# Routing stage of a two-block transformer with experts: order of evictions, exponentials and the gates' table, and wide sums in the last norm

## The chip, the cores and the metric

One core of one Trainium2 chip. The metric is the device time of one execution of the whole program in microseconds, lower is better; several executions are made and their median is taken.

## The reference

512 tokens of width 1024, all in float32. A first block (latent attention with a Fourier branch, then a squared-ReLU MLP) is followed by a second one: a mixer of a convolution and an mLSTM, and a hierarchical mixture of 32 experts, of which each token takes two. The change touches only the seam between the mixer and the experts:

```
h   = x * rsqrt(mean(x*x) + eps) * norm_ffn_g            # the last norm but one
grp = argmax(h @ rg_w + rg_b); p_grp = its softmax value  # 4 groups
top2 of the 8 expert logits of that group
gate = p_grp * softmax(top2)                              # two weights per token
for each expert e, over its tokens xs:
    ys = (silu(xs @ w_gate[e]) * (xs @ w_up[e])) @ w_down[e]
out[token] += gate * ys
y = rmsnorm(x + out)
```

## The kernel before, in words

Every engine has its own program, a hand-written order of instructions, and they wait for each other on counted semaphores. A float32 product is made of three products in a faster form: ScalarE rounds an operand (its high half), VectorE takes the remainder (its low half), and TensorE multiplies high by high, low by high and high by low. Weights are streamed in units of 1 MB: SyncE loads a unit into a raw buffer once VectorE has finished with the unit that was there, `convert(n)` on ScalarE (line 1538) writes its high half, `convert(n)` on VectorE (line 2201) its low half. `use(n)` converts all units up to `n + ahead`. The half buffers are a ring too: a conversion waits until TensorE has used the unit that was in the buffer. From expert 0 on the units come in the order gate 0, up 0, gate 1, down 0, up 1, gate 2, down 1, up 2 and so on, two units each; the expert part is one product stream of 24 (gate), 24 (up) and 24 (down) matmuls of 512 columns per expert.

The seam runs in this order.

- Stage "out2". The mixer's last projection makes xT, the token stream with features on partitions, one block of 128 features (m = 0 to 7) at a time (line 1344). After each block come 4 products for the router's logits (`logits`, line 1363, 36 columns) and 4 for the tokens times the norm's gain, turned to token-major (`gained`, line 1375, 128 columns); ScalarE evicts the latter into hN (line 1590). In the profile each of these float32 products shows as two instructions. `total(12)` (lines 686 and 691) sums the squares over partitions: 8 products of one column, with `oneD` (1/1024) as the moving operand, and ScalarE's `root(12)` (line 1560) takes the root. `token_major(m)` turns xT itself (line 1383): ScalarE copies the eight results into xN (line 1590).
- Stage "route", TensorE: `fill(b, n)` (line 621) is n products of 128 columns with ones whose result nobody reads; then the positions of each token in its expert's list (lines 1412 to 1416), `token_major(3)`, `table(0)` (3 fills, then the table of indices, line 1426), `token_major(4..7)`, and `table(1)`, the table of gates. The PSUM banks are eight in rotation, so the transposes 6 and 7 wait for ScalarE's copies of 0 and 1.
- Stage "route", ScalarE: scales hN by the root's reciprocal in four row blocks and stores each (lines 2091 and 2093, the scratch from which tokens are gathered); loads the exponential's table and takes two exponentials (lines 2095, 2096); converts the second unit of gate 0 and the first of up 0; copies xN; stores xN as the running sum (2 MB, line 2117).
- Stage "route", VectorE: logits, top 2 and one-hot rows (lines 2979 to 3000, many through the helper line 2310), the table's operands R1, the indices `idt`; then the gates' values from the exponentials, converts the second unit of gate 0, counts overflow blocks, and evicts the gates' table.
- Stage "moe": `turn_x(x)` turns the gathered tokens of expert x on TensorE (line 1444), ScalarE copies the high half (line 1590), VectorE takes the low half (line 2310); `half_mm` (line 1460) makes the gate and up products, ScalarE's sigmoid (line 2127) and VectorE make the activations, `turn_a` (line 1469) turns them, `down` (line 1487) multiplies, ScalarE scales by the gate (line 2141), and GpSimd adds the rows to the sum in memory (line 3242). GpSimd also gathers the tokens (line 3231), four experts ahead; the first gather waits for the indices, the stored hN and the norm's reciprocal, the next ones also for transposes 3, 5 and 7.
- SyncE (line 3277) loads in unit order, with extra waits: the second unit of gate 1 waits for gather 0, the first unit of down 0 waits until the stored sum has landed (its buffer lies over xN), and the first load into the fifth raw buffer waits for the gates' table.

```
if n == U_E["g", 1][1]:
    p.wait_ge(*done("dma", "xg", 0))
if n == FIFTH:
    p.wait_ge(*done("dve", "tab", 1))
if n == U_E["d", 0][0]:
    p.wait_ge(*done("dma", "od"))
```

Of the kernel before, what the change touches and what calls it, by code (L numbers as in the profile page):

```python
# [6 lines left out]
F32 = mybir.dt.float32  # L7
# [4 lines left out]
ALU = mybir.AluOpType  # L12
ACT = mybir.ActivationFunctionType
AX = mybir.AxisListType
# [137 lines left out]
class Book:  # L152
# [25 lines left out]
    def done(self, *key):  # L178
        if key == (None,):
            return None, 0  # L180
        if not self.real:
            return None, 0
        name, n = self.value[key]
        return self.sem(name), n
# [74 lines left out]
def build(nc, A, out, ctx):  # L259
# [4 lines left out]
    done = book.done  # L264
# [347 lines left out]
    def pe_program(p):  # L612
        e = p.e
        ps.restart()

        def fill(b, n):

            p.wait_ge(*done("pool", "one"))
            p.wait_ge(*done(*b.before))
            for _ in range(n):  # L620
                e.matmul(b.t[:, 0:128], one1[:, :], one1[:, :], start=True, stop=True)
# [52 lines left out]
        def total(n):  # L674

            width = NORMS[n][1]
            apart = n > 1
            b = ps.take(("norm", n), ("act", "rs", n))
            if n == 0:
                fill(b, 22)  # L680
            p.wait_ge(*done("dve", "sqa", n, 6 if apart else 7))
            p.wait_ge(*done("pool", "one"))
            p.wait_ge(*done(*b.before))
            last = width // 128 - 1
            for i in range(width // 128):
                ins = e.matmul(b.t[:, i:i + 1], sqs[:, i * 128:(i + 1) * 128], oneD[:, 0:1], start=(i == 0),
                               stop=(i == last and not apart))
            if apart:
                p.wait_ge(*done("act", "sq", n, 7))
                for i in range(width // 128):  # L690
                    ins = e.matmul(b.t[:, i:i + 1], scr[:, 1, i * 128:(i + 1) * 128], oneD[:, 0:1], start=False,
                                   stop=(i == last))
            ins.then_inc(*p.inc("sum", n, 7))

# [724 lines left out]
        def table(k, n, vals):  # L1419
            b = ps.take(("tab", k), ("dve", "tab", k))  # L1420
            if k == 0:
                fill(b, 3)
            p.wait_ge(*done("dve", "R", k))
            p.wait_ge(*done(*b.before))
            for c in range(8):
                ins = e.matmul(b.t[:, 0:n], R1[:, c, :], vals[:, c, :], start=(c == 0), stop=(c == 7))
            ins.then_inc(*p.inc("tab", k))
# [2 lines left out]
        table(0, 32, Ot)  # L1430
        for m in range(4, 8):
            token_major(m)
        table(1, 64, Og)


        p.stage("moe")
# [1 line left out]
        def turn_x(x):  # L1438
            for q in range(2):
                b = ps.take(("x4", x, q), ("dve", "xL", x, q))  # L1440
                p.wait_ge(*done("dma", "xg", x))
                p.wait_ge(*done(*b.before))
                for d in range(4):
                    ins = e.transpose(b.t[:, d * 128:(d + 1) * 128], xg[x % NXG][:, (4 * q + d) * 128:(4 * q + d + 1) * 128], ident)  # L1444
                ins.then_inc(*p.inc("x4", x, q))

        def half_mm(x, what, h):
            r = x % 2
            n = U_E[what, x][h]
            u = units[n]  # L1450
            b = ps.take(("e" + what, x), ("dve", what, x)) if h == 0 else ps["e" + what, x]
            if x == 0 and what == "g" and h == 0:
                fill(b, 7)
            p.wait_ge(*done("dve", "xL", x, 1))
            p.wait_ge(*done("dve", "lo", n))
            p.wait_ge(*done(*b.before))
            for k in range(4):
                kk = 4 * h + k
                for i, (l, w) in enumerate(tri((xH[r][:, kk, :], xL[r][:, kk, :]), (u.hi[:, k, :], u.lo[:, k, :]))):
                    ins = e.matmul(b.t[:, :], l, w, start=(kk == 0 and i == 0), stop=(kk == 7 and i == 2))  # L1460
            ins.then_inc(*p.inc("use", n))
# [30 lines left out]
        turn_x(0)  # L1492
        half_mm(0, "g", 0)
        half_mm(0, "g", 1)
        turn_x(1)
        for x in range(NEXP):
            half_mm(x, "u", 0)
# [23 lines left out]
    def act_program(p):  # L1521
# [3 lines left out]
        def convert(n):  # L1525
            u = units[n]
            at_[0] = n + 1
            if not u.split:
                return
            p.wait_ge(*done("dma", "u", n))  # L1530
            for key in u.half_keys:
                p.wait_ge(*done(*key))
            if HOLD.get(n):
                p.wait_ge(*done("pe", HOLD[n]))
            if n in AFTER:
                for key in AFTER[n]:
                    p.wait_ge(*done(*key))
            e.activation(u.hi, u.raw, ACT.Copy).then_inc(*p.inc("hi", n, on="hi"))  # L1538
# [17 lines left out]
        def root(n):  # L1556
            nd, width, _, place = NORMS[n]
            nt = width // 128
            p.wait_ge(*done("pe", "sum", n, nd - 1))
            e.activation(rcol[:, 4 * place:4 * place + nt], ps["norm", n].t[:, 0:nt], ACT.Sqrt, bias=eps[:, :]).then_inc(  # L1560
                *p.inc("rs", n))
# [508 lines left out]
        for m in range(8):  # L2070
# [9 lines left out]
                root_next(12)  # L2080
            if m:
                gained(m - 1)
        root(12)
        gained(7)


# [3 lines left out]
        for i in range(4):  # L2090
            e.activation(hN[:, i, :], hN[:, i, :], ACT.Copy, scale=rcol[:, i:i + 1]).then_inc(*p.inc("hN", i))
            p.wait_ge(*done("act", "hN", i))
            e.dma_start(hd_[i * 128:(i + 1) * 128, :], hN[:, i, :]).then_inc(*p.land("hd", "hd", i))
        p.wait_ge(*done("dve", "ee"))
        e.activation(ee, ee, ACT.Exp).then_inc(*p.inc("ee"))
        e.activation(dd, dd, ACT.Exp).then_inc(*p.inc("dd"))
        convert(U_E["g", 0][1])
        convert(U_E["u", 0][0])
        for m in range(8):
            token_major(m)  # L2100
        p.also("mid")
# [4 lines left out]
        def turn_x(x):  # L2106
            r = x % 2
            for q in range(2):
                p.wait_ge(*done("pe", "x4", x, q))
                if x > 1:  # L2110
                    p.wait_ge(*done("pe", "use", U_E["u", x - 2][1]))
                else:
                    p.wait_ge(*done("pe", "out2", 7))
                copy(xH[r][:, 4 * q:4 * q + 4, :], ps["x4", x, q].t[:, :].rearrange("p (d c) -> p d c", d=4), p.inc("xH", x, q))

        p.wait_ge(*done("act", "xN", 7))
        e.dma_start(od.rearrange("(i p) d -> p i d", p=P), xN[:, :, :]).then_inc(*p.land("od"))
        turn_x(0)
        for n in U_E["g", 0]:
            use(n)  # L2120
        turn_x(1)
# [69 lines left out]
    def dve_program(p):  # L2191
# [3 lines left out]
        def convert(n):  # L2195
            u = units[n]
            at_[0] = n + 1
            if not u.split:
                return
            p.wait_ge(*done("act", "hi", n))  # L2200
            e.tensor_tensor(u.lo, u.raw, u.hi.bitcast(F32), ALU.subtract).then_inc(*p.inc("lo", n, on="lo"))  # L2201
# [104 lines left out]
        def copy(out_, in_, by):  # L2306
            e.tensor_copy(out_, in_).then_inc(*by)

        def TT(out_, a, b, op, *key):
            e.tensor_tensor(out_, a, b, op).then_inc(*p.inc(*key))  # L2310

        def TS(out_, a, s1, s2, op0, op1=None, key=()):
            if op1 is None:
                e.tensor_scalar(out_, a, s1, None, op0).then_inc(*p.inc(*key))
            else:
                e.tensor_scalar(out_, a, s1, s2, op0, op1).then_inc(*p.inc(*key))
# [705 lines left out]
            *p.inc("tab", 0))  # L3022
        p.wait_ge(*p.own())
        copy(idt[:, 0:32], tv[:, 1, :], p.inc("idt"))
        p.wait_ge(*done("act", "dd"))
        e.tensor_reduce(pg, ee, AX.X, ALU.add).then_inc(*p.inc())
        TS(gk[:, 0, :], dd, 1.0, None, ALU.add)
# [9 lines left out]
        copy(Og[:, :, 0:32], Og8, p.inc())  # L3037
        p.wait_ge(*p.own())
        TT(Og[:, :, 32:64], Og8, Og[:, :, 0:32].bitcast(F32), ALU.subtract, "R", 1)
        convert(U_E["g", 0][1])  # L3040
        TS(nov, cnt, 128.5, None, ALU.is_gt)
        for lim in (256.5, 384.5):
            TS(oi, cnt, lim, None, ALU.is_gt)
            p.wait_ge(*p.own())
            TT(nov, nov, oi, ALU.add)
            p.wait_ge(*p.own())
        e.tensor_reduce(ovf[:, 0:1], nov, AX.X, ALU.add).then_inc(*p.inc())
        p.wait_ge(*p.own())
        copy(ovi[:, 8:9], ovf[0:1, 0:1], p.inc("ovi"))
        gates_ = ps["tab", 1].t  # L3050
        p.wait_ge(*done("pe", "tab", 1))
        copy(gsl[:, 0:32], gates_[:, 0:32], p.inc())
        p.wait_ge(*p.own())
        TT(gsl[:, 0:32], gsl[:, 0:32], gates_[:, 32:64], ALU.add, "tab", 1)


        p.stage("moe")
        ahead = 3
        p.stage("moe")
        ahead = 3  # L3060

        def turn_x(x):
            r = x % 2
            for q in range(2):
                p.wait_ge(*done("act", "xH", x, q))
                TT(xL[r][:, 4 * q:4 * q + 4, :], ps["x4", x, q].t[:, :].rearrange("p (d c) -> p d c", d=4),
                   xH[r][:, 4 * q:4 * q + 4, :].bitcast(F32), ALU.subtract, "xL", x, q)

        turn_x(0)
        for n in U_E["g", 0]:  # L3070
            use(n)
        turn_x(1)
        def silu(x):
            r = x % 2
            p.wait_ge(*done("act", "sig", x))
# [527 lines left out]
```

## Time and profile before

| what | value |
|---|---|
| median of 3 executions | 1684.21 us (1683.75 to 1687.3) |
| the profiled execution | 1685.23 us |
| its span, first to last instruction | 1683.4 us |
| mean granted TensorE clock | 0.987 |
| TensorE busy | 1624.3 us (96%) |
| VectorE busy | 1269.6 us (75%) |
| ScalarE busy | 921.3 us (55%) |
| GpSimd busy | 255.3 us (15%) |
| moved by DMA | 322.92 MB, mean 192 GB/s |

All rows come from one profiled execution. Times are microseconds from the start of its span. PE is TensorE's matmuls, PEld its weight loads, DVE is VectorE, ACT ScalarE, POOL GpSimd and SP SyncE. "Granted clock" is the share of TensorE's full 2.4 GHz that the chip granted. Matmuls are pipelined: two that follow each other overlap in the timeline, so a row's duration there is a little longer than its place on the chain of waits. A "releaser" is what the profile infers to have ended a wait. The page divides the span in 40 slices; DMA share is the mean busy share of the core's 16 DMA engines.

### The profile page before, as it was taken

What the parts mean: (1) busy time and instruction counts of PE and PEld (TensorE: products, weight loads), DVE (VectorE), ACT (ScalarE), POOL (GpSimd) and SP (SyncE); (2) the same over time, 40 slices, a digit from 0 to 9 for tenths busy, and PEclk for the clock granted to TensorE, in tenths of its full rate; (3) what the DMA queues carried; (4) which work ended last, traced back from release to release, by engine and by line L of the source; (5) the groups of instructions that cost most, each with busy time, mean ns of one, the idle gap of its engine ahead of it and who ended that gap; (6) DMA issues with size and microseconds to landing.
All of it is one profiled execution on the core that took longest, in us unless ns stands there. A gap on an engine that the chain in (4) does not pass through costs nothing.

```text
span 1683.4 us, 20485 instructions
## 1 busy us (share of the span) xinstructions
PE 1624.3 (96%) x8376; PEld 1332.3 (79%) x8376; DVE 1269.6 (75%) x1457; ACT 921.3 (55%) x1070; POOL 255.3 (15%) x176
## 2 busy tenths in 40 slices
PE   6999999999999999999999999999999999999994
PEld 3768876657988989898888677888888888888883
DVE  6554876777667847474799974589999999999994
ACT  6433235443443625252633234588888887888884
POOL 0000021000028333310000100102112122121200
PEclk9999999999999999999999999899999999999997
DMA  9206821003222313131222111399999999999993
GB/s 381 81 4 242 301 90 76 0 0 126 76 100 76 127 74 129 72 134 67 79 98 76 38 39 56 131 380 414 374 386 369 378 369 369 364 378 363 383 361 115
DMA packets 54484, 322.92 MB, mean 192 GB/s; under 512 B 12529, under 2 KB 13041, under 8 KB 17778
## 3 DMA queue, kind: packets, MB, share of 16 engines
q1 hardware_dynamic: 42192, 304.76, 47.3%
q0 software_dynamic: 9216, 8.43, 2.2%
q10 hardware_dynamic: 2978, 8.37, 1.3%
q8 instruction: 68, 1.11, 0.3%
q14 instruction: 30, 0.25, 0.0%
HBM read 323.60 MB, written 23.07 MB: 206 GB/s over the span
## 4 chain that ended last, share of the span: by engine, by line
PE 87%; DVE 6%; ACT 3%; DMA 3%; issue 1%; POOL 0%; SPq 0%; ACTq 0%; POOLq 0%; DVEq 0%
PE ps L584 25%; PE ps L1460 20%; PE ps L1487 10%; PE ps L1088 7%; PE ps L774 3%; PE ps L750 2%; PE ps L1020 2%; PE ps L1344 2%; DVE scr L2511 2%; PE ps L1444 2%; PE ps L808 1%; ACT whi L1538 1%; DVE wlo L2201 1%; DMA xT<-in_x 1%; PE ps L880 1%
## 5 line engine op out<-in xcount | busy, mean ns | idle before, releaser
L2201 DVE TENSOR_TENSOR wlo<-raw,whi 128x2048 fp32r<-128x2048 f32 x256 | 583.8, 2302 | 129.1 <-ACT whi L1538 129.0
L1538 ACT ACTIVATE whi<-raw 128x2048 fp32r<-128x2048 f32 x256 | 485.7, 1911 | 155.1 <-PE ps L584 40.9
L1460 PE MATMUL ps<-whi,xH 128*128 128x512 f32 x512 | 203.0, 396 | 0.0
L1460 PE MATMUL ps<-whi,xL 128*128 128x512 f32 x512 | 200.3, 391 | 0.0
L1460 PE MATMUL ps<-wlo,xH 128*128 128x512 f32 x512 | 199.6, 390 | 0.0
L584 PE MATMUL ps<-hH,whi 128*128 128x512 f32 x352 | 138.8, 394 | 0.3 <-ACT dmax L2014 0.3
L584 PE MATMUL ps<-hH,wlo 128*128 128x512 f32 x352 | 137.2, 390 | 0.0
L584 PE MATMUL ps<-hL,whi 128*128 128x512 f32 x352 | 137.1, 389 | 0.0
L3242 POOL DMA_INDIRECT sum_scratch<-yb,idt x32 | 51.1, 1596 | 451.2 <-ACT yb L2141 416.9
L1460 PEld LDWEIGHTS ps<-whi,xL 128*128 128x128 f32 x512 | 96.2, 188 | 20.8
L1460 PEld LDWEIGHTS ps<-wlo,xH 128*128 128x128 f32 x512 | 96.4, 188 | 19.2
L1460 PEld LDWEIGHTS ps<-whi,xH 128*128 128x128 f32 x512 | 96.4, 188 | 19.1
L1487 PE MATMUL ps<-whi,aH 128*128 128x512 f32 x256 | 102.3, 400 | 0.6 <-DVE aL L2310 0.6
L1487 PE MATMUL ps<-wlo,aH 128*128 128x512 f32 x256 | 99.8, 390 | 0.0
L1487 PE MATMUL ps<-whi,aL 128*128 128x512 f32 x256 | 99.7, 390 | 0.0
L2773 DVE SCALAR_TENSOR_TENSOR acc<-up,vec,acc 128x512 f32<-128x512 f32 x110 | 82.4, 750 | 2.9
L3231 POOL DMA_INDIRECT xg<-h_scratch,idt x32 | 70.0, 2188 | 94.9 <-DVE gk L2310 84.8
L584 PEld LDWEIGHTS ps<-hH,wlo 128*128 128x128 f32 x352 | 66.1, 188 | 14.1
L584 PEld LDWEIGHTS ps<-hH,whi 128*128 128x128 f32 x352 | 66.1, 188 | 13.9 <-ACT dmax L2014 0.4
L584 PEld LDWEIGHTS ps<-hL,whi 128*128 128x128 f32 x352 | 66.1, 188 | 13.6 <-issue 0.2
L584 PE MATMUL ps<-UH,whi 128*128 128x512 f32 x176 | 68.5, 389 | 0.0
L584 PE MATMUL ps<-UL,whi 128*128 128x512 f32 x176 | 68.5, 389 | 0.0
(517 smaller groups left out, 3542.0 us busy)
## 6 DMA issues: line engine op xcount, KB each, us to landing
raw<-in_experts SPq DMA_DIRECT2D x192, 1024.0 KB, 7.7
raw<-in_streamed SPq DMA_DIRECT2D x92, 1024.0 KB, 4.8
xT<-in_x SPq DMA_DIRECT2D x1, 2048.0 KB, 17.3
h_scratch<-hN ACTq DMA_DIRECT2D x4, 512.0 KB, 2.6
sum_scratch<-xN ACTq DMA_DIRECT2D x1, 2048.0 KB, 13.3
out<-Y SPq DMA_DIRECT2D x4, 512.0 KB, 2.7
ctxT<-in_ctx SPq DMA_DIRECT2D x1, 1024.0 KB, 20.1
Y<-sum_scratch SPq DMA_DIRECT2D x2, 512.0 KB, 5.9
```

Of the source, the lines that this page charges most:

```text
L584: ins = e.matmul(o, l, r, start=(i == 0), stop=(i == len(prs) - 1))
L750: ins = e.matmul(b.t[0:mw, hs(h)], l, r, start=(k == 0 and i == 0), stop=(k == 7 and i == 2))
L774: ins = e.matmul(b.t[:, :], l, r, start=(k == 0 and i == 0), stop=(k == nk - 1 and i == 2))
L1020: ins = e.matmul(b.t[:, :], V[:, j, h // 2, s_:s_ + 2, :].rearrange("p s c -> p (s c)"), PT[h % 2][:, j, :], start=(j == 0), stop=(j == 5))
L1088: ins = e.matmul(bank.t[:, hs(half)], l, r, start=(k == 0 and i == 0), stop=(k == 3 and i == 2))
L1460: ins = e.matmul(b.t[:, :], l, w, start=(kk == 0 and i == 0), stop=(kk == 7 and i == 2))
L1487: ins = e.matmul(bs[q].t[:, :], l, w, start=(kk == 0 and i == 0), stop=(kk == 3 and i == 2))
L1538: e.activation(u.hi, u.raw, ACT.Copy).then_inc(*p.inc("hi", n, on="hi"))
L2201: e.tensor_tensor(u.lo, u.raw, u.hi.bitcast(F32), ALU.subtract).then_inc(*p.inc("lo", n, on="lo"))
L2773: e.scalar_tensor_tensor(out=acc[:, m, :], in0=up[:, m, j:j + 512], scalar=wc, in1=acc[:, m, :], op0=ALU.mult, op1=ALU.add).then_inc(*p.in ...
L3231: e.indirect_dma_start(out=xg[r], out_offset=None, in_=hd_[:, :], in_offset=bass.IndirectOffsetOnAxis(ap=idt[:, x:x + 1], axis=0), bounds_ ...
L3242: e.indirect_dma_start(out=od[:, :], out_offset=bass.IndirectOffsetOnAxis(ap=idt[:, x:x + 1], axis=0), in_=yb[x % 3], in_offset=None, boun ...
```

## The change

Four edits, in the seam only.

1. `total(12)`: the sums of the last norm ahead of the experts are 128 columns wide (every column the same), with `oneK` (1/128) as the moving operand. ScalarE's root reads one column of each 128 and multiplies by 0.125.
2. ScalarE converts only the second unit of gate 0 ahead of the eight copies of xN; the exponentials and the first unit of up 0 come behind the copies of expert 0's turned tokens.
3. VectorE makes the gates' values and evicts their table later: expert 0's low halves go ahead of them; the conversion of the second unit of gate 0 and the count of overflow blocks follow the indices directly.
4. TensorE makes the gates' table behind the gate products of expert 0. Fills: 7 instead of 3 ahead of the indices' table, 9 new ones ahead of expert 0's transposes, 5 instead of 7 ahead of its gate products.

```diff
@@ total(n), TensorE
+            cw, one = (128, oneK[:, :]) if n == 12 else (1, oneD[:, 0:1])
             for i in range(width // 128):
-                ins = e.matmul(b.t[:, i:i + 1], sqs[:, i * 128:(i + 1) * 128], oneD[:, 0:1], start=(i == 0),
+                ins = e.matmul(b.t[:, cw * i:cw * i + cw], sqs[:, i * 128:(i + 1) * 128], one, start=(i == 0),
                                stop=(i == last and not apart))
...
@@ table(k, n, vals), TensorE
             if k == 0:
-                fill(b, 3)
+                fill(b, 7)
...
         for m in range(4, 8):
             token_major(m)
-        table(1, 64, Og)
...
@@ turn_x(x), TensorE
+                if x == 0 and q == 0:
+                    fill(b, 9)
                 p.wait_ge(*done("dma", "xg", x))
...
@@ half_mm, TensorE
             if x == 0 and what == "g" and h == 0:
-                fill(b, 7)
+                fill(b, 5)
...
         turn_x(0)
         half_mm(0, "g", 0)
         half_mm(0, "g", 1)
+        table(1, 64, Og)
         turn_x(1)
@@ ScalarE
-        root(12)
+        p.wait_ge(*done("pe", "sum", 12, 7))
+        e.activation(rcol[:, 0:4], ps["norm", 12].t[:, :].rearrange("p (i c) -> p i c", i=4)[:, :, 0], ACT.Sqrt,
+                     bias=eps[:, :], scale=0.125).then_inc(*p.inc("rs", 12))
...
-        p.wait_ge(*done("dve", "ee"))
-        e.activation(ee, ee, ACT.Exp).then_inc(*p.inc("ee"))
-        e.activation(dd, dd, ACT.Exp).then_inc(*p.inc("dd"))
         convert(U_E["g", 0][1])
-        convert(U_E["u", 0][0])
         for m in range(8):
             token_major(m)
...
         turn_x(0)
+        p.wait_ge(*done("dve", "ee"))
+        e.activation(ee, ee, ACT.Exp).then_inc(*p.inc("ee"))
+        e.activation(dd, dd, ACT.Exp).then_inc(*p.inc("dd"))
         for n in U_E["g", 0]:
             use(n)
         turn_x(1)
@@ VectorE (only the order of the pieces changes)
         copy(idt[:, 0:32], tv[:, 1, :], p.inc("idt"))
+        convert(U_E["g", 0][1])
+        (count of overflow blocks: 8 instructions)
+        turn_x(0)
         p.wait_ge(*done("act", "dd"))
         (the gates' values: 8 instructions, the last makes Og)
-        convert(U_E["g", 0][1])
-        (count of overflow blocks: 8 instructions)
+        for n in U_E["g", 0]:
+            use(n)
+        turn_x(1)
         (eviction of the gates' table: 2 instructions)
-        turn_x(0)
-        for n in U_E["g", 0]:
-            use(n)
-        turn_x(1)
```

## Rows read from the trace of the kernel before

**Rows 1.** Chain of waits from 1055 to 1170 us: start, us, what.

```profile
1066.26 0.97 PE ps L1375 x8
...
1068.02 0.89 PE ps L691 x8
...
1092.69 5.93 PE ps L1460 x24
...
1102.46 10.92 DMA raw<-in_experts
...
1148.24 5.46 PE ps L1487 x24
```

**Rows 2.** Timeline of TensorE: start, us, instruction, count, idle before and its releaser.

```profile
1069.67 2.06 PE L1375 MATMUL ps<-gdiag,xT 128*128 128x128 f32 x8
...
1073.60 3.74 PE L621 MATMUL ps<-one 128*128 128x128 f32 x32
...
1077.17 0.20 PE L1412 MATMUL ps<-AS,triB 128*128 128x32 bf16 x2
...
1080.07 1.07 PE L1426 MATMUL ps<-Ot,R 128*128 128x32 f32 x8 [1.24 <-DVE R L2310]
...
1084.41 1.97 PE L1383 MATMUL ps<-cst,xT 128*128 128x128 f32 x8 [2.33 <-ACT xN L1590]
...
1098.45 1.04 PE L1444 MATMUL ps<-cst,xg 128*128 128x128 f32 x8
...
1130.24 0.50 PE L1487 MATMUL ps<-whi,aH 128*128 128x512 f32 x1 [0.61 <-DVE aL L2310]
```

**Rows 3.** Waits of SyncE's queue, and the store of the sum (KB, us to landing).

```profile
SPq L3277 <- DMA sum_scratch<-xN: 14.3, 1, 14.3
...
sum_scratch<-xN ACTq DMA_DIRECT2D x1, 2048.0 KB, 13.3
```

**Rows 4.** Stretches: us, PE, PEld, DVE, ACT, POOL busy (count), PEclk, DMA share, GB/s.

```profile
1070.00:1072.00 2.00, 2.00 (x11) 2.00 (x11) 1.76 (x11) 0.24 (x1) 0.00 (x0) 0.50 0.00 0
...
1088.00:1090.00 2.00, 2.00 (x11) 2.00 (x11) 0.82 (x3) 0.86 (x2) 1.18 (x2) 0.50 1.01 410
...
1101.00:1102.00 1.00, 1.00 (x6) 0.83 (x5) 1.00 (x1) 0.98 (x3) 0.00 (x0) 1.00 0.00 0
...
1104.00:1110.00 6.00, 6.00 (x30) 4.85 (x29) 5.67 (x5) 5.07 (x4) 0.00 (x0) 1.00 1.01 429
```

**Rows 5.** Timeline of VectorE.

```profile
1076.08 0.29 DVE L2310 TENSOR_TENSOR AS<-O 128x128 bf16<-128x128 f32 x1
...
1081.63 0.18 DVE L2307 CAST idt<-tv 128x32 uint32<-128x32 f32 x1
...
1083.73 2.28 DVE L2201 TENSOR_TENSOR wlo<-raw,whi 128x2048 fp32r<-128x2048 f32 x1
```

**Rows 6.** Timeline of ScalarE.

```profile
1078.67 1.28 ACT L2095 ACT_TABLE_LOAD   x1 [0.39 <-ACT hN L2091]
...
1080.18 3.69 ACT L1538 ACTIVATE whi<-raw 128x2048 fp32r<-128x2048 f32 x2
1083.78 3.98 ACT L1590 ACTIVATE xN<-ps 128x512 f32<-128x512 f32 x8
```

**Rows 7.** The first gather, and landings of the issues at 1082.72 and at 1084.45.

```profile
1082.72 1.43 POOL L3231 DMA_INDIRECT xg<-h_scratch,idt  x1 [84.81 <-DVE gk L2310]
...
DMA to landing us min/median/max: 3.1/3.1/3.1
...
DMA to landing us min/median/max: 12.3/12.3/12.3
```

**Rows 8.** DMA packets of 1084.5 to 1085 (first row), and by queue of 1093 to 1094.

```profile
DMA packets 136, 0.00 MB, mean 9 GB/s; under 512 B 135, under 2 KB 135, under 8 KB 136
...
q1 hardware_dynamic: 29, 0.24, 69.8%
q10 hardware_dynamic: 27, 0.11, 26.8%
```

More of the change, by code:

```diff
@@ L690, in total @@
                 for i in range(width // 128):
-                    ins = e.matmul(b.t[:, i:i + 1], scr[:, 1, i * 128:(i + 1) * 128], oneD[:, 0:1], start=False,
+                    ins = e.matmul(b.t[:, cw * i:cw * i + cw], scr[:, 1, i * 128:(i + 1) * 128], one, start=False,
                                    stop=(i == last))
@@ L3024, in dve_program, with turn_x @@
         copy(idt[:, 0:32], tv[:, 1, :], p.inc("idt"))
+        convert(U_E["g", 0][1])
+        TS(nov, cnt, 128.5, None, ALU.is_gt)
+        for lim in (256.5, 384.5):
+            TS(oi, cnt, lim, None, ALU.is_gt)
+            p.wait_ge(*p.own())
+            TT(nov, nov, oi, ALU.add)
+            p.wait_ge(*p.own())
+        e.tensor_reduce(ovf[:, 0:1], nov, AX.X, ALU.add).then_inc(*p.inc())
+        p.wait_ge(*p.own())
+        copy(ovi[:, 8:9], ovf[0:1, 0:1], p.inc("ovi"))
+        p.stage("moe")
+        ahead = 3
+        p.stage("moe")
+        ahead = 3
+        def turn_x(x):
+            r = x % 2
+            for q in range(2):
+                p.wait_ge(*done("act", "xH", x, q))
+                TT(xL[r][:, 4 * q:4 * q + 4, :], ps["x4", x, q].t[:, :].rearrange("p (d c) -> p d c", d=4),
+                   xH[r][:, 4 * q:4 * q + 4, :].bitcast(F32), ALU.subtract, "xL", x, q)
+        turn_x(0)
         p.wait_ge(*done("act", "dd"))
@@ L3039, in dve_program @@
         TT(Og[:, :, 32:64], Og8, Og[:, :, 0:32].bitcast(F32), ALU.subtract, "R", 1)
-        convert(U_E["g", 0][1])
[L3041 to L3049, printed above, removed]
+        for n in U_E["g", 0]:
+            use(n)
+        turn_x(1)
         gates_ = ps["tab", 1].t
@@ L3054, in dve_program @@
         TT(gsl[:, 0:32], gsl[:, 0:32], gates_[:, 32:64], ALU.add, "tab", 1)
[L3057 to L3067, printed above, removed]
-        turn_x(0)
-        for n in U_E["g", 0]:
-            use(n)
-        turn_x(1)
         def silu(x):
```

## The prediction

> **What bounds it now.** I read the page first: TensorE is busy nearly all of the span, so a gain must take idle or slow time off TensorE, or the transfers that feed it. The change touches only the routing stretch, 1066 to about 1130 us, so I read the chain of waits there. It runs through the first gate products (from 1092.69), then a weight landing of 10.92 us, ScalarE's roundings of weights, and VectorE's lower half of the turned activations, for which the down products of expert 1 wait until 1130.24 [rows 1]. TensorE idles only 0.61 us there [rows 2], and behind it I find no stall: that product's start is where I settle the sum.
>
> Why is a landing on the chain? SyncE stands 14.3 us in front of the first down-weight load, because that load overwrites the token-major sum, whose 2 MB store is issued at 1087.8 and lands 13.3 us later [rows 3]. The four loads behind it go out together from 1101.13. The DMA engines are full at 1088, idle in the microsecond from 1101 (0.00) and then full, at 429 GB/s [rows 4]. So from 1102 on landings come at DMA rate, one load (1.05 MB) in about 2.5 us; an expert's six need 15, its 72 products 16.4 (24 in 5.46 [rows 1]) and the transposes more, so the stream catches up, but not at once. The stream of loads that feeds expert 1 starts when the store has landed, and that sets 1130.24.
>
> TensorE's own loss is ahead of it. Its clock is granted at 0.50 (1.2 GHz) at 1070 to 1072 and again around 1088, at 1.00 (2.4 GHz) later [rows 4]. Eight token transposes take 1.97 us busy at the half level and 1.04 at the full one [rows 2].
>
> **The change, part by part.**
>
> *Wide sums.* 16 one-column products become 128 columns wide. A 128-column run of 8 takes 0.97 us on the chain; the sums take 0.79 (from its end to 1068.02) and 0.89 [rows 1]. So 1.94 replaces 1.68: +0.26 before the root, and as the last logits then run at 0.81 rather than 0.95, +0.12 on VectorE's routing chain. What they may buy is the clock, which falls directly behind them. I take it as held: it fell behind 16 products of one column and recovered under 128-column work, with the fills from 1073.60 at 3.74/32 = 0.12 each [rows 2, 4]. Then the last gain products (2.06 busy) save 0.9 us, the 12 transposes about 0.7, and the 16 filling products end near 1075.9 instead of 1077.17. The position products waited for these fills: their input was ready at 1076.37 [rows 5]. Now they wait for it at 1076.5. Gain on the routing chain 0.6 us, bounds 0.6 gained and 0.3 lost (clock not held). The index table ends at 1081.2 instead of 1081.81. The fills ahead of it grow from 3 to 7, 8 more passes at 0.12, under 1.0 us; TensorE idled 1.24 there [rows 2], so they cost nothing; at the half level they would cost 1.
>
> *VectorE.* The gates' chain, from the index's end at 1081.81 to 1083.73 (the two overlap by 0.1), goes behind the turned tokens, so the low half of the second gate unit starts 2.0 + 0.6 = 2.6 us sooner and ends at 1083.4 [rows 5]. That frees a raw buffer, and SyncE's first load of the pair (now 1086.04) goes out at 1083.5. The second waits for the first gather, due at 1085.2.
>
> *ScalarE.* The row scaling follows the last gain eviction and moves 0.8 us ahead. The table load (1.28) and both exponentials leave, and of two roundings (3.69 together) only one stays: the eight token evictions, 3.98 us from 1083.78, run from 1079.8 to 1083.8 [rows 6]. TensorE can supply them: the last four transposes follow the index table at 1080.5 and no longer wait 2.33 us for a bank [rows 2]. The store of the sum goes out at 1083.8, 3.9 sooner.
>
> *TensorE.* It waits for gather 0. That was issued at 1082.72 and took 3.1 us [rows 7]; 0.6 sooner it lands at 1085.25. 9 fills (2.1 us) cover the wait. Transposes at full clock to 1086.1, ScalarE's two copies (0.60 each) and VectorE's 0.69 behind them give a start of the gate products at 1087.8, against 1092.3. 5 fills (1.2 us) cover that. At 5.46 us for 24 products they end at 1093.25, against 1098.45: 5.2 gained. Now the gates' table comes, about 0.9 at the full level (1.07 busy for the narrower one). Its input needs the exponentials: ScalarE ends its second copy at 1086.9, loads the table and finishes at 1088.5; VectorE's 2.1 us then end at 1090.6, 2.6 before TensorE asks. On TensorE the second expert's transposes and all up products stand behind that wait; on VectorE the up weights' low halves. Who wants the gate values (ScalarE's scaling of the first outputs, SyncE's first load into the fifth raw buffer) asks after 1110, and they are there by 1100. Behind the exponentials stand the roundings of expert 0's up weights; the first unit's low half is ready at 1092.9, needed at 1095. Gather 1, which took 12.3 us behind the same loads [rows 7], should land near 1094, as TensorE reaches it. So the up products start at 1095.0 against 1099.2 (the second expert's transposes begin at 1098.45 [rows 2]): 4.2 gained on TensorE, and without the old stall it would reach the down products of expert 1 at 1125.4.
>
> *The transfers.* They decide between 1125.4 and later. The same four megabytes of weights and sum, and the gathers, must pass before the sum has landed. Their start moves with the first load, by 2.6 us; if the engines stay full the end moves as much. The other bound is the store's own 13.3 us from its issue: 3.9. The load that was second of the pair now follows the store, but with 8 packets per engine against the store's 32 it should be through first if the queues share. I take 2.8, near the first, because rows show the engines full. So the sum lands at 1098.3, the four loads follow, the last lands at 1110.6 instead of 1113.37, and ScalarE and VectorE, whose chain from there is unbroken, deliver at 1127.4.
>
> The rows on sharing: the store's packets begin 4 to 5 us after its issue, behind the weights' queue; at 1093 both run evenly, 29 and 27 packets in one microsecond [rows 8]. The Trainium skill (DMA: Bandwidth & Descriptors, Queues, rings and completion order) says an engine goes round between the queues that have work. The later mix agrees, the late first packet does not, so a transfer that is new to a busy engine seems to wait. By the rule alone a late gather 0 (below) would be served in turn.
>
> **Sum.** TensorE alone 4.8 gained (4.2 and the old 0.6), transfers 2.8: the smaller counts. The profiled execution took 1685.23 us (span 1683.4 and 1.8 around it): 1682.4. The median of the runs, 1684.21, is 1.0 below that execution, so I give 1681.4. TensorE's idle ahead of the down products of expert 1 grows from 0.61 to about 2 (with perhaps 0.5 of it at expert 0's). A measurement here tells a change of about 0.2%, 3.4 us, from none.
>
> **Rivals.**
>
> *A. TensorE is the bound.* If the store passes ahead of the second weight load, it lands 4.8 or more sooner and TensorE arrives last: 4.8 gained, 1679.4. For: the store's issue moves 3.9 and overtakes that load. Against: it has 512 packets of its own behind a busy engine. 20%.
>
> *B. The clock does not hold.* The stretch from 1080 to 1087 still holds narrow table products, transposes and a wait. At the half level the transposes cost 0.9 more, 5 fills 1.1, and the first gate products 1.4: TensorE arrives at 1128.8, gain 1.4: 1682.8. For: it fell in this stretch before, with 2.33 and 1.24 us of idle. Against: the fills. 17%.
>
> *C. Gather 0 is caught by the loads: slower.* It landed in 3.1 us; the next one, behind loads, took 12.3 [rows 7]. Its packets run just before the first load's, which now begin near 1084.9. Caught, it lands at 1094.5; TensorE sits idle, its clock falls, the gate products end at 1104.7 against 1098.45, and with the table's 0.9 behind them and the old 0.61 absorbed the down products start 6.6 later: 1690.8. It decides from a landing about 4.8 us late, or 2 to 3 if the clock falls too; up to 2 late costs nothing. Against: its 144 packets are mostly 4 bytes and were gone in half a microsecond, some 0.5 us ahead of the loads' new start [rows 8]. 8%.
>
> *D. The wide sums do nothing:* the index comes 0.3 later, the stream starts 1.7 sooner instead of 2.6, gain about 1.8, 1682.4. 5%.
>
> **Chances.** Forecast (gain 2.0 to 3.6) 50%. Over 3.4 us lie three tenths of it (15%), most of A (17%) and a little else (2%): faster 0.34. C: slower 0.08. The rest within 0.2%: 0.58. The range runs from A with a little noise, 1679.0, to a loss of 0.8, 1685.0; C and a larger gain are outside.
>
> **What would show it.** Clock 1.00 from 1066 to 1130; position products near 1076.6; the transposes' wait of 2.33 gone; gate products from 1087.8; the store issued near 1083.8 and landed near 1098; DMA share again near zero just ahead of the four loads, at about 1098 instead of 1101; a wait on VectorE's activations of 1 to 2 us at about 1126; behind it 17.7 us per expert as now. Wrong, if the stall stays under 0.7 (A), if a 0.50 stands at 1083 to 1090 (B), or if the first gather takes over 5 us (C).

## The result, and the profile after

The changed kernel is slower: 1688.39 us median of 20 executions (1685.71 to 1690.75) against 1684.46 of 20 of the kernel before, ratio 1.0019 (95% interval 1.0013 to 1.0026), 3 to 4 us. I had forecast 1681.4 and given this side 8%.

The profiled execution's span is 1686.2 us against 1683.4. Its routing stretch begins 0.9 us earlier for reasons ahead of the change, so I compare stretches: from the first of block 6's router logits (1065.28 before, 1064.39 changed) to expert 1's first down product (1130.24 before [rows 2], 1132.88 changed). That is 64.96 us before and 68.49 now, 3.5 more, which is the result. Behind it both kernels run the same 17.7 us per expert.

The timeline of TensorE in the changed kernel (columns as in [rows 2]; line numbers are one to five higher than before):

```profile
1068.78 1.14 PE L1376 MATMUL ps<-gdiag,xT 128*128 128x128 f32 x8
1069.75 1.47 PE L1384 MATMUL ps<-cst,xT 128*128 128x128 f32 x12
1071.06 3.74 PE L621 MATMUL ps<-one 128*128 128x128 f32 x32
1075.50 0.21 PE L1413 MATMUL ps<-AS,triB 128*128 128x32 bf16 x2 [0.70 <-DVE AS L2314]
...
1078.41 1.07 PE L1427 MATMUL ps<-Ot,R 128*128 128x32 f32 x8 [0.34 <-DVE R L2314]
1079.32 1.96 PE L1384 MATMUL ps<-cst,xT 128*128 128x128 f32 x16
1081.12 2.17 PE L621 MATMUL ps<-one 128*128 128x128 f32 x18
1090.65 1.97 PE L1446 MATMUL ps<-cst,xg 128*128 128x128 f32 x8 [7.36 <-DMA xg<-h_scratch,idt]
```

The first half is as forecast: the last gain products take 1.14 us instead of 2.06, the position products now wait 0.70 for their input instead of for the fills, and the wait of 2.33 for a bank is gone. Then TensorE stands 7.36 us in front of gather 0. The chain of waits and, below it, GpSimd's and VectorE's timelines and ScalarE's issue of the store at that place:

```profile
1081.06 9.55 DMA xg<-h_scratch,idt
```

```profile
1081.06 2.41 POOL L3235 DMA_INDIRECT xg<-h_scratch,idt  x1 [84.03 <-PE ps L1384]
1080.06 2.28 DVE L2205 TENSOR_TENSOR wlo<-raw,whi 128x2048 fp32r<-128x2048 f32 x1
1082.71 0.38 ACTq L2118 DMA_DIRECT2D sum_scratch<-xN  x1
```

Gather 0 takes 9.55 us to land instead of 3.1, and GpSimd's instruction for it 2.41 instead of 1.43 [rows 7]. VectorE's low half now stands directly behind the indices and runs beside it. The packets by queue (packets, MB, share of the DMA engines) in the microseconds from 1085, 1087 and 1089 (q1 is SyncE's loads, q10 ScalarE's store, q0 the gathers):

```profile
q1 hardware_dynamic: 42, 0.34, 104.0%
...
q1 hardware_dynamic: 25, 0.13, 49.9%
q10 hardware_dynamic: 32, 0.13, 31.8%
q0 software_dynamic: 11, 0.00, 0.6%
...
q10 hardware_dynamic: 96, 0.39, 95.4%
q0 software_dynamic: 97, 0.00, 6.4%
```

GpSimd is done at 1083.47, yet nothing of gather 0 moves before 1087: first the load's packets, then the gather's in equal number with the store's. Meanwhile the clock falls (the microseconds from 1085 and 1087; columns as in [rows 4], here without the engines):

```profile
1085.00:1086.00 1.00, 1.00 1.04 344
...
1087.00:1088.00 1.00, 0.50 0.82 262
```

So the transposes take 1.97 us again instead of 1.04, and the first gate products run at the half level. They start 30.0 us after the logits' start (1094.40), against 27.1 before: 3.0 of the 3.5 us are lost by then. Behind them TensorE waits for nothing until the down products.

### The profile page after: what moved, and what is told of

Read it like the earlier page. It is cut to its first block, busy times and chain, and to the rows that moved or that the text cites. A ratio compares the mean times of both kernels' runs of the same rounds, so it can differ in the third digit from the quotient of the medians.

```text
span 1686.2 us, 20528 instructions
## 1 busy us (share of the span) xinstructions
PE 1621.0 (96%) x8398; PEld 1331.5 (79%) x8398; DVE 1268.9 (75%) x1457; ACT 920.9 (55%) x1070; POOL 255.0 (15%) x176
## 4 chain that ended last, share of the span: by engine, by line
PE 88%; DVE 6%; DMA 3%; ACT 2%; issue 1%; POOL 0%; SPq 0%; POOLq 0%; DVEq 0%; ACTq 0%
PE ps L584 26%; PE ps L1462 21%; PE ps L1489 10%; PE ps L1089 7%; PE ps L775 3%; PE ps L751 2%; PE ps L1021 2%; PE ps L1345 2%; PE ps L1446 2%; DVE scr L2515 2%; PE ps L809 1%; DMA xT<-in_x 1%; PE ps L1471 1%; PE ps L881 1%; DVE wlo L2205 1%
```

## The experiments

Each kernel was executed 10 or 11 times in turn with the kernel before, except the two that are marked as one execution. "Stretch" is as defined above; the ratios are to the kernel before, with 95% intervals. The first three take away one thing at a time of what stands in front of gather 0.

**Only the load waits.**

```diff
-            if n == U_E["g", 1][1]:
+            if n in U_E["g", 1]:
                 p.wait_ge(*done("dma", "xg", 0))
```

> The changed kernel, but SyncE's first load of gate 1 also waits until gather 0 has landed (the store of the sum still goes out). Theory Q (gather 0 sits behind that load's packets in the DMA engines): gather 0 lands within 5 us of its issue instead of 9.5, TensorE's wait of 7.36 ahead of the first transposes shrinks under 2.5, and the stretch from the last block's logits to expert 1's down products (64.96 us before, 68.49 changed) falls to 62 to 63.5; time 0.1% below the kernel before or equal to it. Rival S (it is the 2 MB store that holds it up): the landing stays over 7 us. Rival P alone (VectorE's long operation only slows GpSimd's writing of descriptors, and nothing stands in front): the landing stays at 9.5 less nothing, since that operation is where it was. Under all of them GpSimd's instruction for gather 0 stays at 2.4 us.

Measured: gather 0 lands 8.9 us after issue, TensorE waits 6.68, stretch 66.34, 1686.37 us, ratio 1.0015 (1.0005 to 1.0024). Theory Q as I put it is wrong: without the load in front, the store alone holds the gather up.

**Only the store waits.**

```diff
         p.wait_ge(*done("act", "xN", 7))
+        p.wait_ge(*done("dma", "xg", 0))
         e.dma_start(od.rearrange("(i p) d -> p i d", p=P), xN[:, :, :])
```

> The changed kernel, but ScalarE's store of the sum waits until gather 0 has landed (the load of gate 1 goes out as in the changed kernel). Theory Q (the load is in front): gather 0 still takes 8 us or more, TensorE's wait stays over 6, and the store lands later, so the stretch stays at 68.5 or grows; time as the changed kernel or 0.1% above. Rival S (the store is in front): the landing falls under 6 us and the stretch under 65.5.

Measured: 6.5 us to landing (1082.83 to 1089.34), TensorE waits 4.29, stretch 65.14, 1685.29 us, ratio 1.0002 (0.9993 to 1.0011). This lies between theories Q and S: each transfer alone holds the gather up, the store by more.

**Both wait** (both edits).

> The changed kernel, with both the load and the store waiting for gather 0. Any queue theory: gather 0 lands 4.0 to 4.5 us after its issue (3.1 of before, and 1.0 to 1.3 for descriptors that are written beside VectorE's long operation), TensorE's wait is 1.5 to 2.2 us, the clock stays at 1.00, and the gate products start 5 us sooner than in the changed kernel. The transfers start when gather 0 lands, about 0.1 us sooner relative to the last logits than before, with the store now first: if the transfers bound the end as I forecast, the stretch is 62.5 to 64.5 and TensorE waits 1 to 3 us ahead of expert 1's down products; if TensorE bounds it (rival A), 60 to 61 with no such wait.

Measured: 4.2 us to landing with GpSimd's instruction still at 2.41, TensorE waits 1.98. That separates the 6.4 us: 1.1 are the slower descriptors, the rest is standing behind the load and the store. Against the changed kernel the stretch is 3.6 shorter, but at 64.87, ratio 1.0010 (1.0001 to 1.0019), nothing is gained on the kernel before, because TensorE now waits on activations further on. (The ratio says up to 3 us more time than before, which the stretch of the one profiled execution does not show.) The clock, expected to stay at 1.00, was at 0.50 from 1089 to 1091. Its waits from 1063 to 1150 in this kernel (us in total, times, longest):

```profile
PE ps L1446 <- DMA xg<-h_scratch,idt: 2.0, 1, 2.0
PE ps L1471 <- DVE ac L2315: 1.6, 1, 1.6
...
PE ps L1489 <- DVE aL L2315: 0.7, 1, 0.7
```

The store landed 13.7 us after its issue and SyncE waited 12.9 for it: the bound that I had forecast for the transfers, in a place where the store goes out late.

**The count first.** Nothing gets a new wait; VectorE makes the eight small operations ahead of the long one.

```diff
         copy(idt[:, 0:32], tv[:, 1, :], p.inc("idt"))
-        convert(U_E["g", 0][1])
         TS(nov, cnt, 128.5, None, ALU.is_gt)
...
         copy(ovi[:, 8:9], ovf[0:1, 0:1], p.inc("ovi"))
+        convert(U_E["g", 0][1])
```

> The changed kernel with one move on VectorE: the count of overflow blocks (8 small instructions, 1.35 us) ahead of the low half of gate 0's second unit, so that this long operation and the load behind it come 1.35 us later. Theory P (VectorE's long operation keeps GpSimd from writing descriptors): GpSimd's instruction for gather 0 falls from 2.41 to 1.0 to 1.6 us, its packets are gone before the load's, and it lands 3.1 to 3.6 us after issue; TensorE's wait falls to about 1, the stretch to 62 to 63. Without P: GpSimd's instruction stays at 2.4, the load is issued at about the time that the descriptors are ready, and the landing is between 4.4 and 8.

Measured: 1680.38 us, ratio 0.9973 (0.9964 to 0.9982), stretch 60.09, faster than both kernels. GpSimd, VectorE, ScalarE's issue of the store, and TensorE there:

```profile
1082.09 1.25 POOL L3235 DMA_INDIRECT xg<-h_scratch,idt  x1 [84.05 <-DVE nov L2314]
1083.65 1.85 POOL L3235 DMA_INDIRECT xg<-h_scratch,idt  x1 [0.30 <-issue]
1082.34 2.27 DVE L2205 TENSOR_TENSOR wlo<-raw,whi 128x2048 fp32r<-128x2048 f32 x1
1083.74 0.38 ACTq L2118 DMA_DIRECT2D sum_scratch<-xN  x1
1085.24 1.09 PE L1446 MATMUL ps<-cst,xg 128*128 128x128 f32 x8 [0.91 <-DMA xg<-h_scratch,idt]
```

Gather 0 lands in 3.1 us, the clock stays at 1.00, and TensorE has no wait on activations at all: SyncE stands 7.5 us for the store's landing instead of 14.3 [rows 3]. Two things changed at once: the descriptors, and the first load, which goes out at 1084.64, 2.55 us behind gather 0 instead of 1.31.

The long operation still runs beside gather 0's instruction here, for 1.0 of its 1.25 us, and costs it nothing: it began 0.25 us later than GpSimd. Gather 1's instruction began while it ran, and took 1.85 instead of about 1.0.

**What slows the descriptors: two inputs or one** (one execution each). Both put a long VectorE operation back between the indices and the count; only its inputs differ. The first repeats the subtraction (two inputs in SBUF), the second takes a maximum of the raw weights (one input); their results are overwritten or unused, and the real low half comes about 2.2 us later in both.

```diff
+        g01 = units[U_E["g", 0][1]]
+        p.wait_ge(*done("act", "hi", g01.n))
+        e.tensor_tensor(g01.lo, g01.raw, g01.hi.bitcast(F32), ALU.subtract).then_inc(*p.inc())
```

```diff
+        e.tensor_reduce(ovf[:, 1:2], g01.flat, AX.X, ALU.max).then_inc(*p.inc())
```

> The kernel with the count first, and directly behind the indices VectorE makes the low half of gate 0's second unit once more (the same two-input subtraction of 128x2048, its result overwritten by the real one, which with its load comes 2.3 us later). Theory P (a long VectorE operation with two inputs in SBUF keeps GpSimd from writing descriptors): GpSimd's instruction for gather 0 goes from 1.25 back to 2.3 to 2.4 us, its packets then meet the store's, and it lands 7 to 9 us after issue, as where only the load waited (8.9); TensorE waits 5 us or more. Without P: 1.25 us, and 3.1 to landing.

> As the run with the subtraction made twice, but the extra VectorE operation is a maximum over the same 128x2048 raw weights: one input in SBUF, about as long (2.2 us), its result not used. Theory P in the form 'two inputs': GpSimd's instruction stays at 1.0 to 1.3 us, gather 0 lands 3.1 us after issue, TensorE waits under 1 us. If any long VectorE operation does it: 2.3 us and 7 to 9 to landing, as in the other run.

Measured: two inputs, 8.8 us to landing, stretch 66.40, 1688.68 us; one input, 3.6 us, stretch 60.40, 1679.35 us. VectorE, GpSimd and TensorE, with two inputs and then with one:

```profile
1083.15 2.28 DVE L3031 TENSOR_TENSOR wlo<-raw,whi 128x2048 fp32r<-128x2048 f32 x1
1084.16 2.40 POOL L3238 DMA_INDIRECT xg<-h_scratch,idt  x1 [84.06 <-PE ps L1384]
1093.05 1.97 PE L1446 MATMUL ps<-cst,xg 128*128 128x128 f32 x8 [6.65 <-DMA xg<-h_scratch,idt]
```

```profile
1080.03 2.28 DVE L3031 TENSOR_REDUCE ovf<-raw 128x1 f32<-128x2048 f32 x1
1081.03 1.25 POOL L3238 DMA_INDIRECT xg<-h_scratch,idt  x1 [84.06 <-PE ps L1384]
1084.65 1.09 PE L1446 MATMUL ps<-cst,xg 128*128 128x128 f32 x8 [1.37 <-DMA xg<-h_scratch,idt]
```

The two operations are equally long and stand at the same distance ahead of GpSimd's (1.0 us). With two inputs GpSimd needs 1.15 us more, and those 1.15 us are enough for the store's packets to be first. This is the cleanest pair of the study: the store goes out 1.65 us after the gather's issue in both, and the load 4.75 us after it, behind the landing with one input, and with two inputs too late for its packets to matter (they begin at 1092.8, the gather lands at 1093.0).

One execution each is little, but the other traces agree. In all eleven, 12 of GpSimd's gather instructions began while a subtraction of 2.3 us with two inputs in SBUF ran. Gather 0's five ended 1.12 to 1.13 us after the subtraction did, the seven of later gathers 0.87 to 0.89 us after it; without such an operation running at its start, gather 0's takes 1.25 us (1.43 beside a shorter one with two inputs) and a later one 1.0. So GpSimd's work seems to begin about when the subtraction ends.

**The wide sums alone** on the kernel before, with the root that goes with them.

```diff
+            cw, one = (128, oneK[:, :]) if n == 12 else (1, oneD[:, 0:1])
-                ins = e.matmul(b.t[:, i:i + 1], sqs[:, i * 128:(i + 1) * 128], oneD[:, 0:1], start=(i == 0),
+                ins = e.matmul(b.t[:, cw * i:cw * i + cw], sqs[:, i * 128:(i + 1) * 128], one, start=(i == 0),
```

> The kernel before with the wide sums and the root that goes with them, and nothing else of the change. Theory W (they hold the clock): granted clock 1.00 at the last gain products, the position products start 0.6 us sooner relative to the last logits, and with them all of the seam: the stretch to expert 1's down products is 64.96 less 0.6, 64.2 to 64.6, time 0 to 0.05% below before. Rival (nothing else follows, because the next drop of the clock and the weights' landings keep their place): 64.9, time the same. If the clock falls behind the sums as before: 65.2.

Measured: clock 1.00 from 1066 to 1078, stretch 63.76 (down products at 1129.38, logits at 1065.62), 1683.94 us, ratio 0.9995 (0.9986 to 1.0004). The profile shows 1.2 us, twice what I expected; the timed runs can't tell it from nothing. The second half of it is the clock further on: the granted clock is back at 1.00 from 1091, 25.4 us after the logits' start, and in the kernel before from 1094, 28.7 after it, so the filling products ahead of the gate products take 2.57 us instead of 3.19 and the gate products start 25.6 us after the logits' start instead of 27.1. Why the half level ends sooner stays open.

**The count first, with narrow sums.**

```diff
-            cw, one = (128, oneK[:, :]) if n == 12 else (1, oneD[:, 0:1])
+            cw, one = (1, oneD[:, 0:1])
```

with the root of before in place of the one that reads every 128th column.

> The kernel with the count first (stretch 60.09, ratio 0.9973), with the one-column sums and the root of before. Theory W: the clock falls behind the sums, the position products start 0.6 to 0.8 us later, the stretch is 60.8 to 61.2 and the ratio to before 0.9977 to 0.998. If the clock then stays at 0.50 into the index table (7 fills at the half level) it is 61.5 to 62. Rival: no effect beyond 0.2 us.

Measured: stretch 60.81, 1680.94 us, ratio 0.9980 (0.9971 to 0.9989): 0.72 us for the wide sums by the profile, as expected; the ratio's interval overlaps that of the kernel with the wide sums. The clock at that place (window, us, PEclk, DMA share, GB/s):

```profile
1068.00:1070.00 2.00, 0.97 0.03 8
1070.00:1072.00 2.00, 0.50 0.00 0
1072.00:1074.00 2.00, 0.68 0.00 0
```

It falls without the wide sums and stays up with them, in both pairs of kernels.

**The count first, the store behind gather 0** (the edit of the second run on the kernel of the fourth).

> The kernel with the count first (stretch 60.09, no wait of TensorE on activations), and ScalarE's store of the sum waits until gather 0 has landed, which puts it behind the first load of gate 1 and level with the second, the order that my forecast's term for the transfers assumed. Theory T (the store's place among the loads decides when it lands, and its landing starts the stream that feeds expert 1): gather 0 still lands in 3.1 us, the gate products start where they did, but the store lands 12 to 13.5 us after its issue, SyncE waits 10 us or more for it instead of 7.5, and TensorE waits 1.5 to 3 us on VectorE's activations between 1118 and 1130; the stretch is 61.8 to 63.5, the ratio to before 0.998 to 0.9993. Rival (TensorE is the bound whatever the store does): 60.1 and no such wait, ratio 0.9973.

Measured: gather 0 lands in 3.2 us, TensorE's first waits are unchanged (0.98 and 0.46), but the store lands 13.5 us after its issue, and TensorE waits later on:

```profile
PE ps L1471 <- DVE ac L2315: 1.7, 1, 1.7
PE ps L1489 <- DVE aL L2315: 1.2, 2, 0.7
```

SyncE's wait is

```profile
SPq L3282 <- DMA sum_scratch<-xN: 13.2, 1, 13.2
```

The stretch is 63.66, just above what theory T allowed; 1685.15 us, ratio 1.0002 (0.9993 to 1.0011). The stretch is 1.3 us shorter than before and the timed runs show none of it; a gain of 1.3 us lies at the very edge of their interval. Against the fourth run the store's place alone costs 3.6 us of stretch.

## Why the prediction was wrong

**The step that failed is the landing of gather 0.** The sum put it at 1085.25, 20.0 us after the logits' start, by moving the 3.1 us of [rows 7] to the new issue. It landed at 1090.61, 26.2 after the start, and the gate products, put at 22.5, began at 30.0. This was rival C, gather 0 caught by the loads, with the right place and mechanism. Its price was too high (6.6 us, measured 3.5) because it took gather 1's 12.3 us to landing, and its chance far too low, 8%, on the ground that the gather's packets were gone 0.5 us ahead of the loads' new start.

My working moved the load and the gather as if they were independent. But the same edit puts VectorE's long two-input operation next to GpSimd's descriptor writing: the descriptors are ready at 1083.47. With the 1.25 us of the other runs they would have been ready at 1082.3, and the first packet came 0.6 us behind them wherever the DMA engines were free. That makes 1082.9, an estimate, and the load's first packet moved at 1083.34: the margin of 0.5 was there, and the 1.16 us used it up. The store's first packet, 1.65 us behind the gather's issue, is decided by this alone (the pair of one execution each); for the load no run has quick descriptors with the load as close, so that it would have stayed behind is not shown.

The kernel before had the warning, in the instruction of its gather 1 and the subtraction beside it, and in small in gather 0's 1.43:

```profile
1082.60 0.42 DVE L2310 TENSOR_TENSOR e<-O,gk 128x256 f32<-128x256 f32 x1
1083.73 2.28 DVE L2201 TENSOR_TENSOR wlo<-raw,whi 128x2048 fp32r<-128x2048 f32 x1
1084.45 2.44 POOL L3231 DMA_INDIRECT xg<-h_scratch,idt  x1 [0.30 <-issue]
```

Gather 0's instruction, begun at 1082.72, ended 1.13 us after the short operation that was running; gather 1's ended 0.88 us after the long one. I had also looked only at the load as the obstacle, though my own working moved the store 3.9 us forward; the first run shows that the store alone holds the gather to 8.9 us.

The Trainium skill has this (SBUF — State Buffer, "SBUF: two separate sides"): VectorE and GpSimd share a port pair as an exclusive lock, whichever starts first has it for its whole instruction, and a VectorE operation with two SBUF inputs takes it only against a GpSimd operation that reads SBUF. The gather reads its indices from SBUF, and the traces agree: 2.40 us with two inputs against 1.25 with one, and 1.25 again where GpSimd began first. That it is this port pair, no run here shows. I did not weigh that page. The page of the Trainium skill that I did weigh (DMA: Bandwidth & Descriptors, "Queues, rings and completion order") speaks of going round between queues with work; of what came first the traces show otherwise: gather 0's first packet waited from 1083.47 to after 1087, and only then was it one of the gather's to one of the store's (97 and 96 in the microsecond from 1089).

**The transfers' term (2.8 us) was mis-sized, and had the order wrong.** I assumed that the store still ends last in a full stretch of the DMA engines, moved by the start of the first load. In the changed kernel the second load stood behind gather 0 until 1090.62, and the first down load, which waits for the store's landing, went out at 1094.30, 29.9 us after the logits' start instead of 35.8: 5.9 sooner. So the stall that I forecast is absent there too. Where gather 0 is not caught (the count first), the store goes out at 1083.74, ahead of both loads, and lands 10.0 us later: 28.3 us after the logits' start, so 7.5 sooner. Then TensorE is the bound, which was rival A: 4.8 gained, said there; 4.9 of stretch and 4.5 us of time (ratio 0.9973) measured. With the store put behind, the stall of my forecast is there (1.7 and 1.2 us in all). So the forecast's mechanism is real, but its condition did not hold.

**Right, by the steps.** The wide sums hold the clock: 1.00 through 1066 to 1086, and worth 0.7 us in the pair (0.6 forecast); they lengthen the sums by 0.1 us, not 0.26 (the last logits start 3.57 us after block 6's instead of 3.49). The index table ends at 1080.14, 15.75 after the logits' start, against 16.53 before: 0.8 (0.6). The first load goes out 2.8 us sooner relative to the start (2.6), the store, at 1082.71, 4.2 sooner (3.9). The fills ahead of the index table cost nothing (TensorE idles 0.34). In the kernel with the count first TensorE's own path is where I put it: gate products 22.5 us after the logits' start (22.5 forecast), the second expert's transposes at 1094.54, which waited some 0.2 for gather 1, and no wait for the gates' table.

**What the change cost**, then: about 8.4 us of stretch between 60.09 and 68.49 hang on where one VectorE instruction stands. 1.1 of them are descriptors; the rest is the queueing that these let in, with the load 1.25 us closer, and the clock that fell in TensorE's idle time. How the rest divides between load, store and clock no run separates fully.

## What to carry to other kernels

A transfer that everyone waits for, issued through GpSimd, wants two things around it: no long two-input VectorE operation running when GpSimd begins on its descriptors, and no bulk transfer, on any queue, whose packets begin before those descriptors are written. Here a store issued 1.65 us behind the gather cost it at most 0.5 us when the descriptors took 1.25 us, and more than 5 when they took 2.40. When a buffer is freed sooner, ask which small transfer the load that follows will now overtake. And of two bulk transfers, the one whose landing releases the next loads goes first: the store ahead of the weights was worth 3.6 us of stretch here, once the gather was clear.

## What I had not expected of the hardware

- A gather of 144 packets, nearly all of 4 bytes, lands in 3.1 us on free DMA engines and in 6.5, 8.9 and 9.5 us behind a load, a store and both, of which 1.1 us each time are slower descriptors. Its first packet comes 2.9, 3.7 and 4.0 us after its descriptors are written, and 0.6 us after them on free engines.
- A VectorE operation of 2.28 us that began 1.0 us ahead lengthened GpSimd's descriptor writing from 1.25 to 2.40 us with two inputs in SBUF. With one input the instruction took 1.25 us, as it did where the two-input operation began 0.25 us behind it and ran beside the rest.
- The same 2 MB store takes 10.0 us to land when it is issued 0.9 us ahead of the first of two weight loads, and 13.1 to 13.7 us when it is issued together with the first or up to 1.8 us behind it. It took 7.7 us when no load went out in the 3 us behind it (three runs).
